# RMSNorm roots with the tokens on partitions, spread by identity matmuls, in a two-layer decoder step on one Trainium2 core

## The chip, the core and the metric

The kernel runs as one launch on one core of one Trainium2 chip. The metric is the device time of the launch in microseconds. Engines: PE is TensorE's matmul (PEld its weight load), DVE is VectorE, ACT is ScalarE, POOL is GpSimd, SP issues the weight transfers.

## The reference, cut to what matters

One step of a two-layer decoder on 320 tokens (256 of a prompt, 64 of eight samples) with D = 2048 features:

```python
def _rmsnorm(x, g):
    y = xf * lax.rsqrt(jnp.mean(xf * xf, axis=-1, keepdims=True) + RMS_EPS)
    return (y * g.astype(jnp.float32)).astype(x.dtype)

def _ffn_sublayer(h, norms_l, w_in, w_out):
    return h + _rmsnorm(_swiglu(_rmsnorm(h, norms_l[2]), w_in, w_out), norms_l[3])

# layer 0
h = h + _rmsnorm(mix, norms_l[1])            # causal pooling mixer
h = _ffn_sublayer(h, norms_l, w_in, w_out)
# shared K/V, then layer 1
kv = _rmsnorm(h, kv_norm) @ w_kv
h = h + _rmsnorm(out, norms_l[1])            # sparse attention, out = o @ w_o
h = _ffn_sublayer(h, norms_l, w_in, w_out)
```

Every sublayer's output is normed before it is added to the residual stream h (a post-norm), and the sum is normed again for the next projection (a pre-norm).

## The kernel before

Features lie on the 128 partitions, in KT = 16 chunks; the NT = 320 tokens lie on the free axis. A projection is made in tiles of 128 output features: for each chunk three fp32r matmuls of 128x320 with the high and low parts of activations and weights (x_hi·w_hi, x_lo·w_hi, x_hi·w_lo; lines 1395 to 1397). SP loads weight panels of 128x2048 into two slots; ACT makes each panel's high part (hi_split, line 492), DVE its low part (lo_split, line 812). The high split of a panel waits until PE has left the panel two before it, which has the same slot. Every engine runs its queue in the order written; semaphores tie them together.

The work around the change is a norm boundary: a post-norm and, behind it, the pre-norm of the next projection. There are three: after the pooling mixer (norms 1 and 2), after the first FFN (3 and 4, ahead of K/V) and after W_O (5 and 6, ahead of the second FFN). Norm 7 ends the kernel. A boundary goes so:

- POOL adds the squares of the 16 output chunks y to acc (line 1282). PE sums them over the partitions with a matrix of ones (acc_sum, lines 1437 to 1442) into PSUM bank STAT, so each of the 128 partitions holds the sums of all 320 tokens. ACT takes the root (rms_root, line 512), DVE the reciprocal (rms_recip, line 820), both of 128x320. In two boundaries PE runs 18 f32 matmuls of 128x128 meanwhile (stay_warm, line 1405).
- For each chunk DVE multiplies y by gain and r (line 850) and adds it to h (line 838). With lag = 1 the add of a chunk stands behind the next chunk's multiplication. ACT then writes x_hi and h times the gain (lines 516 and 598), POOL x_lo (line 1289). All of this is in the unnormed scale: the next projection is multiplied by the pre-norm's r only at its output.
- PE begins at once: four tiles together, chunk by chunk (group, lines 1407 to 1426), 12 matmuls a chunk, one panel for four chunks. I call these panels 1 to 4, and the next two tiles, made in the ordinary way by after_group, the fifth and sixth panel (`tile(c + 4)` and `tile(c + 5)`).
- Meanwhile ACT squares the new h (line 524) and DVE sums the squares (line 864) into acc and r. PE sums these two over the partitions inside the fifth tile, behind its fourth chunk (pre_sum, lines 1444 to 1448), ACT takes the root, DVE the reciprocal. The first readers of r are the FFN's gates (line 1029; ACT's silu, line 536, follows) or the K/V outputs (line 1095). The seventh tile needs the PSUM bank that those reads give back.

The order that matters is written by hand: post_and_pre on ACT (when each panel's high split and each square comes), post_norm on DVE (after which add each low split comes), after_group on PE.

Of the kernel before, what the change touches and what calls it, by code (L numbers as in the profile page):

```python
# [29 lines left out]
P = 128  # L30
# [96 lines left out]
def build(nc, x, st, gains, consts, onehot, rel, w_pool, w_in0, w_in1, w_out0, w_out1, w_kv, w_q, w_o, flips,  # L127
# [86 lines left out]
    pgs = at("pgs", "S", [1, NP_ALL], I32)  # L214
    ident = cst[:, C_ID:C_ID + P]
# [5 lines left out]
    STAT = 7  # L221

    def group_banks(c):

        return 1 - c % 2, 2, 3, 4

    def r_post(c):
# [24 lines left out]
                                                                       "root_made", "r_made"))  # L252
    yn_made, h_made, hacc_made, hg_made = sem("yn_made"), sem("h_made"), sem("hacc_made"), sem("hg_made")
# [228 lines left out]
    def _(act):  # L482
# [108 lines left out]
        def post_and_pre(a, m, k, g, c):  # L591
# [15 lines left out]
            rms_root(m + 1)  # L607

# [188 lines left out]
    def _(dve):  # L797
# [20 lines left out]
        def rms_recip(m, dst=r[:, :]):  # L818
            dve.wait_ge(root_made, m + 1)
            V.reciprocal(dst, root[:, :]).then_inc(r_made, 1)  # L820
            dve.wait_ge(r_made, m + 1)
# [7 lines left out]
        def post_norm(a, m, g, c):  # L829
# [5 lines left out]

            def add(i):
# [9 lines left out]
            rms_recip(m, r_post(c))  # L846
            for i in range(KT):
                if i > lag:
                    dve.wait_ge(h_made, KT * a + i - lag)
                V.scalar_tensor_tensor(out=t_add(i), in0=y[:, i, :], scalar=gn[:, g, i:i + 1],  # L850
                                       in1=r_post(c), op0=ALU.mult, op1=ALU.mult).then_inc(yn_made, 1)
                if i >= lag:
# [3 lines left out]

            for i in range(2, KT):
                if i == 8:
                    lo_split(c + 4, 0)
                dve.wait_ge(sq_made, 16 * m + i + 1)  # L860
                if i >= 4:
                    dve.wait_ge(hacc_made, (KT - 2) * a + i - 3)
# [1003 lines left out]
```

## Time and profile before

| | |
|---|---|
| time, median of 3 runs | 2569.56 us (2568.44 to 2571.85) |
| the profiled execution | 2569.97 us, its span 2568.4 us |
| TensorE busy | 2508.5 us, 98% of the span |
| VectorE busy | 1203.5 us, 47% |
| ScalarE busy | 924.1 us, 36% |
| GpSimd busy | 267.6 us, 10% |
| mean granted TensorE clock | 0.995 |

The share of an engine is its busy time over the span. A wait is shown in the timeline in square brackets behind the instruction it delayed, with the releaser: `[1.88 <-DVE r L864]` is 1.88 us of idling that ended when line 864 on DVE was done. The granted clock is a share of 2.4 GHz; the other level, 1.2 GHz, shows as 0.50.

### The profile page before, as it was taken

The page shows a single profiled execution, that of the slowest core. Times are in us where ns is not written, and L with a number is a line of the kernel's source. Part 1 is how long each engine was busy: PE and PEld are TensorE (multiplying, and loading weights), DVE is VectorE, ACT ScalarE, POOL GpSimd, SP SyncE. Part 2 cuts the span into 40 slices and gives each one's busy share as a digit, 9 for nine tenths or more (in the row PEclk, how much of TensorE's full clock was granted, in tenths as well). Part 3 has the DMA queues.
Part 4 walks back from the last instruction along what each step waited for, and adds up shares of the span by engine and source line. Part 5 has one row for each costly group of instructions (what it writes and reads, how often), then busy time and mean ns, then how long its engine had stood idle before and what let it go on. Part 6 is the DMA issues. An engine that isn't in the chain of part 4 may idle for free.

```text
span 2568.4 us, 43982 instructions
## 1 busy us (share of the span) xinstructions
PE 2508.5 (98%) x17310; PEld 2463.1 (96%) x17310; DVE 1203.5 (47%) x1361; ACT 924.1 (36%) x1154; POOL 267.6 (10%) x316
## 2 busy tenths in 40 slices
PE   6999999999999999999999999999999999999997
PEld 6899999999999999999998799899999999999997
DVE  7564444444444444644534743744444444444444
ACT  4554223323332333532324643633233233323332
POOL 0420000000000001300002311300000000000012
PEclk9999999999999999999999999999999999999998
DMA  6434444344444444456445464344444444444443
GB/s 246 164 131 147 156 162 152 135 162 163 147 155 157 151 153 152 134 159 177 157 165 180 167 185 155 115 147 160 162 147 151 151 159 147 147 162 151 152 149 127
DMA packets 89481, 400.64 MB, mean 156 GB/s; under 512 B 13788, under 2 KB 24428, under 8 KB 59858
## 3 DMA queue, kind: packets, MB, share of 16 engines
q1 hardware_dynamic: 79202, 379.92, 43.9%
q0 software_dynamic: 6160, 12.60, 1.5%
q10 hardware_dynamic: 4064, 7.42, 0.8%
q8 instruction: 31, 0.51, 0.1%
q14 instruction: 24, 0.20, 0.0%
HBM read 392.16 MB, written 19.02 MB: 160 GB/s over the span
## 4 chain that ended last, share of the span: by engine, by line
PE 89%; DVE 5%; ACT 3%; issue 1%; SPq 1%; POOL 1%; DMA 0%; DVEq 0%; ACTq 0%
PE ps L1395 27%; PE ps L1397 27%; PE ps L1396 27%; PE ps L1480 2%; ACT w_hi L492 1%; DVE w_lo L812 1%; PE ps L1649 1%; PE ps L1575 1%; ACT y L598 0%; ACT x_hi L516 0%; PE ps L1646 0%; POOL sc L1360 0%; PE ps L1679 0%; SPq L367 0%; ACT sq L524 0%
## 5 line engine op out<-in xcount | busy, mean ns | idle before, releaser
L1395 PE MATMUL ps<-x_hi,w_hi 128*128 128x320 f32 x3536 | 1095.4, 310 | 5.9 <-DVE sg L1029 2.4
L1396 PE MATMUL ps<-x_lo,w_hi 128*128 128x320 f32 x3536 | 1093.2, 309 | 0.0
L1397 PE MATMUL ps<-x_hi,w_lo 128*128 128x320 f32 x3536 | 1093.1, 309 | 0.0
L812 DVE TENSOR_TENSOR w_lo<-w_raw,w_hi 128x2048 fp32r<-128x2048 f32 (+1 forms) x362 | 744.5, 2057 | 651.3 <-ACT w_hi L492 651.3
L492 ACT CAST w_hi<-w_raw 128x2048 fp32r<-128x2048 f32 (+1 forms) x362 | 618.7, 1709 | 515.4 <-PE ps L1397 479.7
L1395 PEld LDWEIGHTS ps<-x_hi,w_hi 128*128 128x128 f32 x3536 | 664.6, 188 | 8.1 <-issue 3.0
L1396 PEld LDWEIGHTS ps<-x_lo,w_hi 128*128 128x128 f32 x3536 | 664.6, 188 | 0.5 <-issue 0.4
L1397 PEld LDWEIGHTS ps<-x_hi,w_lo 128*128 128x128 f32 x3536 | 664.4, 188 | 0.0
L1397 PE MATMUL ps<-hid_hi,w_lo 128*128 128x320 f32 x1408 | 435.1, 309 | 0.0
L1395 PE MATMUL ps<-hid_hi,w_hi 128*128 128x320 f32 x1408 | 435.1, 309 | 0.0
L1396 PE MATMUL ps<-hid_lo,w_hi 128*128 128x320 f32 x1408 | 435.1, 309 | 0.0
L1395 PEld LDWEIGHTS ps<-hid_hi,w_hi 128*128 128x128 f32 x1408 | 264.4, 188 | 0.0
L1396 PEld LDWEIGHTS ps<-hid_lo,w_hi 128*128 128x128 f32 x1408 | 264.4, 188 | 0.0
L1397 PEld LDWEIGHTS ps<-hid_hi,w_lo 128*128 128x128 f32 x1408 | 264.4, 188 | 0.0
L1301 POOL TENSOR_TENSOR hid_lo<-hb,hid_hi 128x320 f32 x88 | 77.4, 880 | 1586.5 <-ACT hid_hi L540 1586.5
L540 ACT CAST hid_hi<-hb 128x320 f32 (+1 forms) x88 | 40.4, 459 | 408.3 <-DVE hb L1037 408.3
L536 ACT ACTIVATE sg<-sg 128x320 f32<-128x320 f32 x88 | 41.6, 473 | 385.2 <-DVE sg L1029 385.0
L1055 DVE TENSOR_TENSOR y<-y,ps 128x320 f32 (+1 forms) x128 | 62.5, 488 | 201.0 <-PE ps L1397 201.0
L1029 DVE TENSOR_TENSOR sg<-ps,r 128x320 f32<-128x320 f32 x88 | 43.2, 491 | 153.5 <-PE ps L1397 153.4
L1037 DVE TENSOR_TENSOR hb<-sg,ps 128x320 f32<-128x320 f32 x88 | 42.9, 488 | 133.7 <-PE ps L1397 133.0
L503 ACT ACTIVATE sq<-y 128x320 f32<-128x320 f32 x48 | 22.7, 472 | 176.0 <-DVE y L1055 97.3
L1282 POOL TENSOR_TENSOR acc<-acc,sq 128x320 f32<-128x320 f32 x60 | 56.0, 933 | 239.2 <-ACT sq L503 211.6
(253 smaller groups left out, 1471.8 us busy)
## 6 DMA issues: line engine op xcount, KB each, us to landing
w_raw<-w_in_dram SPq DMA_DIRECT2D x176, 1024.0 KB, 4.9
w_raw<-w_out_dram SPq DMA_DIRECT2D x128, 704.0 KB, 4.0
w_raw<-w_kv_dram SPq DMA_DIRECT2D x24, 1024.0 KB, 6.4
w_raw<-w_q_dram SPq DMA_DIRECT2D x17, 1024.0 KB, 4.9
w_raw<-w_o_dram SPq DMA_DIRECT2D x15, 1024.0 KB, 5.5
win_out_dram<-win_kv_dram POOLq DMA_DIRECT2D x8, 992.0 KB, 5.4
rowsK<-cmp_data_dram SPq DMA_DIRECT2D x16, 256.0 KB, 7.1
rowsV<-cmp_data_dram SPq DMA_DIRECT2D x16, 256.0 KB, 4.0
```

The lines of the kernel that those rows point to most:

```text
L492: nc.scalar.copy(w_hi[:, slot, 0:width], src).then_inc(hi_made, 1)
L536: A(sg[:, :], sg[:, :], ACT.Silu).then_inc(silu_made, 1)
L812: V.tensor_tensor(w_lo[:, slot, 0:width], src, w_hi[:, slot, 0:width].bitcast(F32), ALU.subtract).then_inc(lo_made, 1)
L1029: V.tensor_tensor(sg[:, :], ps[:, banks[0], 0:NT], r[:, :], ALU.mult).then_inc(bank_read[c % 2], 1)
L1037: V.tensor_tensor(hb[:, :], sg[:, :], ps[:, banks[1], 0:NT], ALU.mult).then_inc(bank_read[(c + 1) % 2], 1)
L1055: V.tensor_tensor(y[:, n, :], y[:, n, :], ps[:, (o + j) % 2, 0:NT], ALU.add).then_inc(bank_read[(o + j) % 2], 1)
L1282: G.tensor_tensor(acc[:, :], acc[:, :], sq[:, i % 2, :], ALU.add).then_inc(acc_made, 1)
L1301: G.tensor_tensor(hid_lo[:, i, :], hb[:, :], hid_hi[:, i, :].bitcast(F32), ALU.subtract).then_inc(hid_made, 1)
L1395: M(out, wh, xh[:, k, :], start=(k == 0), stop=False)
L1396: M(out, wh, xl[:, k, :], start=False, stop=False)
L1397: last = M(out, wl, xh[:, k, :], start=False, stop=(k == kt - 1))
L1480: return M(ps[:, bank + j // CS, half * w:(half + 1) * w], w1[:, j, :], rows[:, :, j % CS, :], start=(j % CS == 0), stop=(j % CS == CS - 1))
```

## The change

The sums over partitions are turned round: acc (or sq, or r) of 128 tokens becomes the stationary operand and one column of ones the moving one, so that a sum of squares lands with its token on a partition. The 320 tokens need three such thirds (starting at tokens 0, 128 and 192), each one column: root and reciprocal are then of 128x3. To have r on all partitions again, PE multiplies: each of the three columns, broadcast as the stationary operand, with the identity (across_rows, 128 + 128 + 64 columns). For the pre-norms ACT copies the result from PSUM into r (r_kept), which the readers now wait for. Of the 18 matmuls of stay_warm, 4 stand ahead of the spread and 10 behind it, in another bank.

Besides, the first chunk is added before the second is multiplied; ACT's squares and splits and DVE's splits and sums are put in another order; PE sums the squares of the pre-norm behind the eighth chunk of the fifth tile and spreads r behind the twelfth. In the first boundary the spread stands among the matmuls of the block compression.

```diff
+    THIRDS = 0, P, NT - P
+    def third_sum(m):
+        return ps[:, STAT - 2:STAT + 1, 0:1] if m % 2 and m > 1 else ps[:, STAT, NT:NT + 3].unsqueeze(2)
...
         def rms_root(m):
             act.wait_ge(stat_made, m + 1)
-            A(root[:, :], ps[:, STAT, 0:NT], ACT.Sqrt, bias=epsc[:, 0:1], scale=1.0 / D).then_inc(root_made, 1)
+            dst, src = (rootT, third_sum(m)[:, :, 0]) if m else (root[:, :], ps[:, STAT, 0:NT])
+            A(dst, src, ACT.Sqrt, bias=epsc[:, 0:1], scale=1.0 / D).then_inc(root_made, 1)
...
                 A(y[:, i, :], h[:, i, :], ACT.Copy, scale=gn[:, g, i:i + 1]).then_inc(hg_made, 1)
+                if i == 2:
+                    squares_pre(a, 0, 3)
+                if i == 3:
+                    squares_pre(a, 3, 4)
+                if i == 6:
+                    hi_split(c + 2, 0)
                 if i == 9:
-                    hi_split(c + 2, 0)
+                    squares_pre(a, 4, 6)
+                if i == 10:
+                    hi_split(c + 3, 0)
                 if i == 13:
-                    hi_split(c + 3, 0)
-            squares_pre(a, 0, 8)
-            hi_split(c + 4, 0)
-            squares_pre(a, 8, KT)
+                    hi_split(c + 4, 0)
+            squares_pre(a, 6, KT)
             hi_split(c + 5, 0)
             rms_root(m + 1)
+            act.wait_ge(rb_made, m + 1)
+            nc.scalar.copy(r[:, :], ps[:, STAT, 0:NT]).then_inc(r_kept, 1)
...
                 if i == 2:
                     lo_split(c + 1, 0)
-                if i == 11:
+                if i == 8:
                     lo_split(c + 2, 0)
-                if i == 15:
+                    square_sums(2, 4)
+                if i == 12:
                     lo_split(c + 3, 0)
...
+            rms_recip(m)
+            dve.wait_ge(rb_made, m)
+            normed(0)
+            add(0)
+            for i in range(1, KT):
+                normed(i)
                 if i > lag:
                     add(i - lag)
             if lag:
                 add(KT - 1)
...
+            lo_split(c + 4, 0)
+            square_sums(4, KT)
+            rms_recip(m + 1)
             lo_split(c + 5, 0)
-            rms_recip(m + 1)
+            dve.wait_ge(r_kept, a + 1)
...
             def sums(k):
-                if k == 4:
+                if k == 8:
                     pre_sum(m)
+                if k == 12:
+                    across_rows(m, STAT)
...
+        def across_rows(m, bank):
+            pe.wait_ge(r_made, m + 1)
+            done = 0
+            for n, t in enumerate(THIRDS):
+                last = M(ps[:, bank, done:t + P], rT[:, n:n + 1].broadcast_to([P, P]), ident[:, done - t:P],
+                         start=True, stop=True)
+                done = t + P
+            last.then_inc(rb_made, 1)
...
-            M(ps[:, STAT, 0:NT], ones[:, :], acc[:, :], start=True, stop=False)
-            M(ps[:, STAT, 0:NT], ones[:, :], r[:, :], start=False, stop=True).then_inc(stat_made, 1)
+            for n, t in enumerate(THIRDS):
+                M(third_sum(m)[:, n], acc[:, t:t + P], ones[:, 0:1], start=True, stop=False)
+                last = M(third_sum(m)[:, n], r[:, t:t + P], ones[:, 0:1], start=False, stop=True)
+            last.then_inc(stat_made, 1)
...
-        values(0, 20, CB)
+        values(0, 20, 24)
+        pe.wait_ge(b1_made, 2)
+        across_rows(1, P_FFN0 % 2)
+        values(0, 24, CB)
         values(1, 0, CB).then_inc(cmp_sum, 1)
         ffn(P_FFN0, 0, 2, 0)
         acc_sum(3)
-        stay_warm(18)
+        stay_warm(4)
+        across_rows(3, P_KV % 2)
+        stay_warm(10)
         group(P_KV, 1)
...
         ffn(P_FFN1, 3, 6, HT)
         acc_sum(7)
+        across_rows(7, 0)
```

What this moves, at three places. First PE at the second boundary, from the post-norm's sum to the first matmul of the group (cst holds the identity, rt the three columns of root and reciprocal). Before:

```order
L1440 MATMUL ps<-acc,ones 128x320 [waits acc_made]
L1442 MATMUL ps<-sq,ones 128x320 [waits sq_made]
L1405 MATMUL ps<-ones 128x128 x18
L1420 MATMUL ps<-x_hi,w_hi 128x320 [waits xhi_made,lo_made]
L1420 MATMUL ps<-x_hi,w_hi 128x320 x3
```

Now:

```order
L1473 MATMUL ps<-ones,acc 128x1 [waits acc_made]
L1473 MATMUL ps<-ones,acc 128x1 x2
L1478 MATMUL ps<-ones,sq 128x1 [waits sq_made]
L1478 MATMUL ps<-ones,sq 128x1 x2
L1435 MATMUL ps<-ones 128x128 x4
L1486 MATMUL ps<-cst,rt 128x128 [waits r_made]
L1486 MATMUL ps<-cst,rt 128x128
L1486 MATMUL ps<-cst,rt 128x64
L1435 MATMUL ps<-ones 128x128 x10
L1450 MATMUL ps<-x_hi,w_hi 128x320 [waits xhi_made,lo_made]
```

PE now waits for DVE's reciprocal in the middle of its warm-up, and the ten matmuls behind the spread stand ahead of the group.

Then ACT at the end of the same boundary, from the last chunk on. Before:

```order
L516 ACTIVATE x_hi<-h,gn 128x320 [waits h_made]
L598 ACTIVATE y<-h,gn 128x320
L524 ACTIVATE acc<-h 128x320
L524 ACTIVATE r<-h 128x320
L524 ACTIVATE sq<-h 128x320 x2
L524 ACTIVATE sq<-h 128x320 [waits hacc_made] x4
L492 CAST w_hi<-w_raw 128x2048 [waits tile_made,raw_in0]
L524 ACTIVATE sq<-h 128x320 [waits hacc_made] x8
L492 CAST w_hi<-w_raw 128x2048 [waits tile_made,raw_in1]
```

Now:

```order
L525 ACTIVATE x_hi<-h,gn 128x320 [waits h_made]
L607 ACTIVATE y<-h,gn 128x320
L533 ACTIVATE sq<-h 128x320 [waits hacc_made] x10
L500 CAST w_hi<-w_raw 128x2048 [waits tile_made,raw_in1]
L521 ACTIVATE rt<-ps,few 128x3 [waits stat_made]
L624 COPY r<-ps 128x320 [waits rb_made]
```

Ten squares are left behind the last chunk instead of sixteen, and the fifth panel's split, before between them, now stands ahead of the last two chunks; the copy of r stands ahead of whatever ACT does for the next projection.

Last DVE in the same boundary, the middle of the new order (the rows of before have no split between the third chunk and the twelfth):

```order
L872 TENSOR_TENSOR h<-h,ps 128x320 [waits yn_made]
L829 TENSOR_TENSOR w_lo<-w_raw,w_hi 128x2048 [waits hi_made]
L868 TENSOR_TENSOR acc<-acc,sq 128x320 [waits sq_made]
L868 TENSOR_TENSOR r<-r,sq 128x320 [waits sq_made]
L859 SCALAR_TENSOR_TENSOR ps<-y,gn,ps 128x320 [waits h_made]
```

The third panel's low split stands behind the ninth chunk's add, with two sums of squares, and the chunks that follow queue behind them.

## Rows read from the trace of the kernel before

**Rows 1.** The page: busy time of each engine; the chain that ended last.

```profile
PE 2508.5 (98%) x17310; PEld 2463.1 (96%) x17310; DVE 1203.5 (47%) x1361; ACT 924.1 (36%) x1154; POOL 267.6 (10%) x316
...
PE 89%; DVE 5%; ACT 3%; issue 1%; SPq 1%; POOL 1%; DMA 0%; DVEq 0%; ACTq 0%
```

**Rows 2.** Timeline, second boundary: start, duration (us), engine, operation, count [wait <-releaser].

```profile
1054.28 0.81 PE L1442 MATMUL ps<-sq,ones 128*128 128x320 f32 x2 [0.73 <-ACT sq L503]
1054.65 4.26 PEld L1405 LDWEIGHTS ps<-ones 128*128 128x128 f32 x36
1055.12 0.53 ACT L512 ACTIVATE acc<-ps,few 128x320 f32<-128x320 f32 x1 [0.90 <-PE ps L1442]
...
1055.68 2.16 DVE L820 RECIPROCAL ps<-acc 128x320 f32<-128x320 f32 x1 [1.96 <-ACT acc L512]
...
1060.02 0.83 PE L1420 MATMUL ps<-x_hi,w_hi 128*128 128x320 f32 x4 [0.92 <-ACT x_hi L516]
```

**Rows 3.** Single lines over the span: duration ns min/median/max, starts, forms.

```profile
L1214 DVE RECIPROCAL rec<-tot x24: 167/172/193, 1382.9 to 1484.1; 128x6 f32<-128x6 f32 x16, 128x3 f32<-128x3 f32 x8
...
L508 ACT ACT_TABLE_LOAD  x5: 1283/1283/1283, 1.4 to 2475.9; - x5
L508 ACT ACTIVATE few<-few x5: 202/203/203, 2.7 to 2477.2; 128x1 f32<-128x1 f32 x5
...
L1494 PE MATMUL ps<-ones,brow x4: 167/208/250, 53.4 to 97.8; 128*128 128x1 f32 x4
```

**Rows 4.** Timeline: two low parts on POOL, one sum of squares on DVE.

```profile
112.75 0.87 POOL L1289 TENSOR_TENSOR x_lo<-y,x_hi 128x320 fp32r<-128x320 f32 x1 [0.24 <-ACT y L598]
...
1627.26 2.07 POOL L1289 TENSOR_TENSOR x_lo<-y,x_hi 128x320 fp32r<-128x320 f32 x1 [1.83 <-ACT y L598]
...
1083.39 1.17 DVE L864 TENSOR_TENSOR r<-r,sq 128x320 f32<-128x320 f32 x1
```

**Rows 5.** Timeline, PE: the fifth and sixth tile of the second boundary.

```profile
1090.27 0.41 PE L1395 MATMUL ps<-x_hi,w_hi 128*128 128x320 f32 x1 [0.51 <-DVE w_lo L812]
...
1094.17 1.08 PE L1447 MATMUL ps<-acc,ones 128*128 128x320 f32 x2 [1.88 <-DVE r L864]
...
1102.23 0.31 PE L1395 MATMUL ps<-x_hi,w_hi 128*128 128x320 f32 x1
...
1109.12 0.31 PE L1397 MATMUL ps<-x_hi,w_lo 128*128 128x320 f32 x1
```

**Rows 6.** Windows: PE, PEld, DVE, ACT, POOL busy (instructions), clock, DMA share, GB/s.

```profile
1096.00:1097.00 1.00, 1.00 (x5) 0.89 (x4) 1.00 (x1) 0.53 (x1) 0.00 (x0) 0.50 0.00 0
1649.00:1650.00 1.00, 1.00 (x4) 0.71 (x3) 1.00 (x1) 0.13 (x1) 0.00 (x0) 0.50 0.00 0
```

**Rows 7.** Timeline, third boundary: fifth tile, its sums, first read of r, seventh tile.

```profile
1643.52 0.42 PE L1395 MATMUL ps<-x_hi,w_hi 128*128 128x320 f32 x1 [0.52 <-DVE w_lo L812]
...
1647.41 1.36 PE L1447 MATMUL ps<-acc,ones 128*128 128x320 f32 x2 [1.87 <-DVE r L864]
...
1653.04 0.49 DVE L1029 TENSOR_TENSOR sg<-ps,r 128x320 f32<-128x320 f32 x1
...
1663.76 0.42 PE L1395 MATMUL ps<-x_hi,w_hi 128*128 128x320 f32 x1 [1.04 <-DVE sg L1029]
```

**Rows 8.** Timeline, first boundary: third panel's split, fifth tile, r's first reader, later tiles.

```profile
126.15 1.91 ACT L492 CAST w_hi<-w_raw 128x2048 fp32r<-128x2048 f32 x1 [9.03 <-PE ps L1425]
...
147.02 0.31 PE L1395 MATMUL ps<-x_hi,w_hi 128*128 128x320 f32 x1
...
155.08 0.49 DVE L1029 TENSOR_TENSOR sg<-ps,r 128x320 f32<-128x320 f32 x1
...
155.61 0.47 ACT L536 ACTIVATE sg<-sg 128x320 f32<-128x320 f32 x1 [2.94 <-DVE sg L1029]
...
164.47 0.42 PE L1395 MATMUL ps<-x_hi,w_hi 128*128 128x320 f32 x1 [1.36 <-DVE sg L1029]
...
179.78 0.41 PE L1395 MATMUL ps<-x_hi,w_hi 128*128 128x320 f32 x1 [0.95 <-DVE w_lo L812]
```

More of the change, by code:

```diff
@@ L816, in tile_wait, with rms_recip @@
             dve.wait_ge(tile_made, half * 2 + (c + TOFF + 1))
-        def rms_recip(m, dst=r[:, :]):
+        def rms_recip(m):
             dve.wait_ge(root_made, m + 1)
-            V.reciprocal(dst, root[:, :]).then_inc(r_made, 1)
-            dve.wait_ge(r_made, m + 1)
+            if m:
+                V.reciprocal(rT, rootT).then_inc(r_made, 1)
+            else:
+                V.reciprocal(r[:, :], root[:, :]).then_inc(r_made, 1)
+                dve.wait_ge(r_made, m + 1)
         def x_low(k, g, i):
@@ L834, in t_add, with normed, square_sums @@
                 return ps[:, STAT - i % 2 * lag, 0:NT]
+            def normed(i):
+                if i > lag:
+                    dve.wait_ge(h_made, KT * a + i - lag)
+                V.scalar_tensor_tensor(out=t_add(i), in0=y[:, i, :], scalar=gn[:, g, i:i + 1],
+                                       in1=r_post(c), op0=ALU.mult, op1=ALU.mult).then_inc(yn_made, 1)
+            def square_sums(lo, hi):
+                for i in range(lo, hi):
+                    dve.wait_ge(sq_made, 16 * m + i + 1)
+                    if i >= 4:
+                        dve.wait_ge(hacc_made, (KT - 2) * a + i - 3)
+                    total = (acc, r)[i % 2][:, :]
+                    V.tensor_tensor(total, total, sq[:, i % 2, :], ALU.add).then_inc(hacc_made, 1)
             def add(i):
@@ L855, in post_norm @@
                 add(KT - 1)
[L857 to L862, printed above, removed]
-                total = (acc, r)[i % 2][:, :]
-                V.tensor_tensor(total, total, sq[:, i % 2, :], ALU.add).then_inc(hacc_made, 1)
+            lo_split(c + 4, 0)
+            square_sums(4, KT)
+            rms_recip(m + 1)
             lo_split(c + 5, 0)
-            rms_recip(m + 1)
+            dve.wait_ge(r_kept, a + 1)
         def last_norm(a, m, g):
-            rms_recip(m, r_post(0))
+            rms_recip(m)
+            dve.wait_ge(rb_made, m)
             t_add = ps[:, STAT, 0:NT], ps[:, STAT - 1, 0:NT]
@@ L1404, in stay_warm @@
             for _ in range(n):
-                M(ps[:, 5, 0:P], ones[:, :], ones[:, :], start=True, stop=True)
+                M(ps[:, 4, 0:P], ones[:, :], ones[:, :], start=True, stop=True)
         def group(c, k):
@@ L1439, in acc_sum @@
             pe.wait_ge(acc_made, KT * (m // 2 + 1))
-            M(ps[:, STAT, 0:NT], ones[:, :], acc[:, :], start=True, stop=False)
+            for n, t in enumerate(THIRDS if m > 1 else ()):
+                M(third_sum(m)[:, n], acc[:, t:t + P], ones[:, 0:1], start=True, stop=False)
             pe.wait_ge(sq_made, KT * m)
-            M(ps[:, STAT, 0:NT], ones[:, :], sq[:, (KT - 1) % 2, :], start=False, stop=True).then_inc(stat_made, 1)
+            for n, t in enumerate(THIRDS):
+                if m == 1:
+                    M(third_sum(m)[:, n], acc[:, t:t + P], ones[:, 0:1], start=True, stop=False)
+                last = M(third_sum(m)[:, n], sq[:, (KT - 1) % 2, t:t + P], ones[:, 0:1], start=False, stop=True)
+            last.then_inc(stat_made, 1)
[7 more added lines that the diff above has]
+            last.then_inc(rb_made, 1)
         def pre_sum(m):
             pe.wait_ge(hacc_made, (KT - 2) * (m // 2))
-            M(ps[:, STAT, 0:NT], ones[:, :], acc[:, :], start=True, stop=False)
-            M(ps[:, STAT, 0:NT], ones[:, :], r[:, :], start=False, stop=True).then_inc(stat_made, 1)
+            for n, t in enumerate(THIRDS):
+                M(third_sum(m)[:, n], acc[:, t:t + P], ones[:, 0:1], start=True, stop=False)
+                last = M(third_sum(m)[:, n], r[:, t:t + P], ones[:, 0:1], start=False, stop=True)
+            last.then_inc(stat_made, 1)
         def x_ready(k):
@@ L1752, in _ @@
         acc_sum(5)
-        stay_warm(18)
+        stay_warm(4)
+        across_rows(5, P_FFN1 % 2)
+        stay_warm(10)
         ffn(P_FFN1, 3, 6, HT)
         acc_sum(7)
+        across_rows(7, 0)
     block_ctx.close()
```

9 lines of the change are left out of this document (3 added, 6 removed).

## The prediction

> **What bounds the kernel now.** Read first the busy times and the chain that ended last [rows 1]: TensorE works for 98% of the span and makes 89% of the chain, so the other engines cost time only where TensorE waits for them. The windows and the timeline show where: in four norms. Of a post-norm and the pre-norm behind it (I call the pair a boundary) there are three, and one post-norm ends the kernel. So the sum has four terms, each read from its own stage. A change of 0.2% is 5.1 us, and a measurement of this kernel tells no less from no change.
>
> **Prices.** The reciprocal of 128x320 takes 2.16 us [rows 2]; of 128x3 it takes 0.17 [rows 3]. The square root of 128x320 takes 0.53 [rows 2], ScalarE's smallest operation 0.20 [rows 3]; I take 0.24 for 128x3. An f32 matmul loads its weights twice: 36 loads of warm-up last 4.26 us [rows 2], 0.118 each with the tail of the last; I take 0.116. The f32 matmuls of one column last 0.17 to 0.25 each by their rows [rows 3], so 0.08 to 0.125 a load: the bounds. Three matmuls are 0.70 us (0.5 to 0.75), six 1.39 (1.0 to 1.5). Copying the spread root, 128x320, costs as the 0.53 root.
>
> **Second boundary (after the first FFN, ahead of K/V).** Before, the root's sum is there at 1055.09, the root ends at 1055.65, the reciprocal at 1057.84, and the first matmul of the group starts at 1060.02 [rows 2]. Now: sum (0.70 + 0.15 tail) at 1055.1 again, root and reciprocal done at 1055.6, four warm-up matmuls until 1055.9, the spread 0.70 + 0.15, so r at 1056.7: 1.15 earlier. Adding the first chunk at once, not behind the second's 0.46, makes it 1.6; less 0.15 for one hand-over more, 1.45. But the ten other warm-up matmuls hold TensorE for 20 x 0.116 = 2.3 us, to 1058.9. The group starts 1.1 earlier. Its next stop is chunk 1's low part, which GpSimd makes behind VectorE's split of the second panel; that split begins 1.0 earlier, so 1.0 is kept.
>
> Inside the group the splits of panels 3, 4 and 5 move ahead among the chunks. A low part alone takes 0.87; one that begins during a split took 2.07 [rows 4], 1.2 more, and ends 0.74 behind the split. I followed the new order through the group with these durations and TensorE's 1.76 a chunk (12 matmuls at 0.1466). ScalarE reaches the fourth panel behind chunk 10, VectorE's half ends at 1080.35, so low part 11 is ready at 1081.09; TensorE wants it at 1080.7, 0.4 late. The fifth panel's split ends at 1086.39 and holds low part 14 to 1087.13, wanted at 1086.4: 0.8 late. Before, both panels were split behind those chunks and neither low part was late. The moved sums of squares 2 and 3 meet GpSimd too: one such sum took 1.17 [rows 4], and of that I count 0.3 inside the 0.4. The Trainium skill, in "SBUF — State Buffer", section "🔬 SBUF: two separate sides", says that a VectorE instruction with two SBUF inputs and a GpSimd one lock each other out whole. By it both sums could be held a full low part, an estimate of 2 x 0.87 = 1.7 us with the row's duration, and this term would be 1.4 worse.
>
> In return the fifth panel's split is due long before its tile: the wait of 0.51 and 0.2 of stalls at 1090.27 go [rows 5]. The tile starts at -1.0 + 1.2 - 0.7 = 0.5 earlier. Of its two tiles' 96 matmuls the last starts 1109.12 - 1090.27 = 18.85 behind the first; at the pitch of the undisturbed sixth tile, (1109.12 - 1102.23)/47 = 0.1466 [rows 5], that would be 13.93. The 4.9 between are the wait of 1.88, the sums and what follows them. The windows show that [rows 6]: the granted clock is 0.50, 1.2 GHz, behind the wait. Less 1.88 and about 1.3 for the sums at full clock, 1.7 are the fall's. Now the squares are made among the chunks, their sums stand at about 1092.5, and TensorE asks for them after eight chunks (1089.8 + 3.5 = 1093.3): no wait, no fall. Sums of 1.39 and a spread of 0.70 stand in place of the 4.9, so 2.8 less. **Term: -3.3.**
>
> **Third boundary (after W_O, ahead of the second FFN).** The tile again starts 0.5 earlier. Before, the FFN's first read of r came 1653.04 - 1643.52 = 9.52 behind it [rows 7], with the wait of 1.87 and a fall like the other's. Now it comes after eight chunks 3.52 + sums 1.39 + four chunks 1.76 + spread 0.70 + tail 0.15 + copy 0.53 = 8.05: 1.5 earlier. The work from that read to the seventh tile (1663.76 - 1653.04 = 10.72, all on VectorE and ScalarE) stays, so the tile resumes 2.0 earlier. But TensorE reaches it 14.08 (96 matmuls) + 1.39 + 0.70 = 16.17 after the fifth's start and waits until 8.05 + 10.72 = 18.77: the wait grows from 1.04 to 2.6. Waits of 1.88 and 1.87 were followed by the half clock, one of 1.36 was not [rows 5, 7, 8]; so I expect a new fall, +1.7. **Term: -0.3**; -2.0 if the clock holds.
>
> **First boundary (pooling layer, ahead of the first FFN).** VectorE's saving is hidden: TensorE is busy with compression matmuls until the group starts. It gets 0.70 of spread, and 0.2 for the sum, whose 1.39 stand against two matmuls of 320 columns (one lasts 0.81 [rows 2], and they overlap): +0.9. ScalarE stands for 9.03 us at the third panel's split, at 126.15 [rows 8], until TensorE has left the first panel. It stood there after ten chunks, now after seven, with all that is behind it in its queue. That makes the same two low parts late, by 0.5 and 0.9: +1.4. The tile of 147.02 starts 2.3 later. r follows 8.05 behind it, as before (155.08 - 147.02 = 8.06). But the gate's table load of 1.28 [rows 3] and its activation, before at 155.61, 0.53 behind the first read [rows 8], now stand behind the copy of r: 1.28 between copy and activation, +0.75. The seventh tile resumes +3.0 after 164.47, with its wait up from 1.36 to 2.1. If the clock falls there, 1.7 more is mostly taken up by the wait of 0.95 at 179.78. **Term: +3.0** (2.0 to 4.0).
>
> **End.** The last normalisation stands behind root 0.53 and reciprocal 2.16, as in rows 2. Now 0.24 + 0.17 + 0.85 for the spread and two hand-overs of 0.1 stand there: **-1.2**. The square-root table doesn't move; the weight transfers keep their order on SP's queue and can only start earlier, with the splits that free their slots.
>
> **Sum.** -3.3 - 0.3 + 3.0 - 1.2 = -1.8 against the profiled execution's 2569.97, which gives 2568.2; the median of the runs, 2569.56, is 0.4 lower, which would give 2567.8. The forecast between them is **2568.0 us**: no change that can be measured.
>
> **Rivals.** *Low parts in time* (faster). If GpSimd and VectorE miss each other, the three lots of 1.2 to 1.4 in the groups go (3.9), and the third boundary's clock holds (1.7): 2568.0 - 5.6 = 2562.4. For it: in the trace only some low parts are held. Against: the splits are closer together now. Chance 0.25.
>
> *One-column matmuls don't hold the clock* (slower). They keep TensorE loading weights while few columns pass. If such stretches are as idle to the clock as a wait, it falls behind the sums of both later post-norms and of three pre-norms: 5 x 1.7 = 8.5, 2576.5. [...] Against: by themselves they are no longer than the 1.36 after which the clock stayed [rows 8]. The Trainium skill ("TensorE: Matmul & The Clock Gate", section "🔬 Part 1: The HAM clock gate") says that recent activity of the array sets the clock; no row here shows what a one-column matmul counts for. Chance 0.08.
>
> *It doesn't do what it says*: the squares still end late, because ScalarE stands at the third panel's split, and TensorE waits at the sums for a microsecond with the clock's fall kept. Then the wait of about 1 and the fall's 1.7 are back in the second boundary, 2.7 (the third has its new fall in the sum already): 2570.7. My margin there is only 0.7 us. Chance 0.17.
>
> **How the numbers follow.** Forecast 0.5, rivals 0.25, 0.08 and 0.17. The range takes in the first and third rival and the bounds of the loads (+-0.4 in each of four terms) and of the first boundary: 2562.0 to 2573.0. Faster by over 0.2% (below 2564.4) is the first rival, 0.25; slower (above 2574.7) the second, 0.08; the rest 0.67.
>
> **What would show it.** Right: no wait for sums of squares in the second and third boundary and a granted clock of 1.00 behind them; waits on GpSimd's low parts near chunks 11 and 14 of each group; a wait of 2.6 and then 0.50 at the seventh tile of the third; the last norm starting 1.2 nearer to its sum. Wrong: a fall of the clock behind one-column sums, a wait at them, a spread that takes over 0.9, or groups without late low parts.

## The result: 0.14% slower, and the profile after

The changed kernel takes 2574.16 us (median of 18 runs, 2571.81 to 2577.51) against 2570.35 for the kernel before in the same runs: a ratio of 1.0014, 95% interval 1.0008 to 1.0021, so 2 to 5 us more. It is slower, by less than the 0.2% that the prediction took as its bound, and 1.2 us above the range's end of 2573.0. The execution that was profiled is the slowest of the 18, 2577.51 us: its stages below add up to 5.9 us more than those of before, while the medians differ by 3.8.

To compare executions I cut each profile at four places: the *first* boundary runs from the post-norm's first sum to the seventh tile, the *second* from the last chunk's sum to the first matmul behind the sixth tile, the *third* from the last chunk's sum to the seventh tile, the *end* from the last chunk's sum to the end of the span. What lies between is the same in both kernels (first FFN 889.8, K/V to W_O 498.15, second FFN 888.4 us), and what lies ahead of the first sum, where all kernels here are the same, differs by up to 5 us between executions (95.7 to 100.9), so profiled spans alone mislead.

| us | first | second | third | end |
|---|---|---|---|---|
| before | 66.56 | 55.08 | 56.25 | 16.26 |
| after | 71.51 | 56.55 | 57.05 | 14.98 |
| difference | +4.95 | +1.47 | +0.80 | -1.28 |
| predicted | +3.0 | -3.3 | -2.0 | -1.2 |

The prediction's -0.3 for the third boundary is -2.0 up to the seventh tile and a fall of the clock, +1.7, behind it. Only the end went as forecast. The first boundary of the kernel after, in its timeline (start, duration, engine, operation, count, and in brackets the wait and what ended it; rows of several engines together):

```profile
131.60 3.15 POOL L1319 TENSOR_TENSOR x_lo<-y,x_hi 128x320 fp32r<-128x320 f32 x2 [15.49 <-ACT y L607]
...
132.85 1.17 DVE L868 TENSOR_TENSOR acc<-acc,sq 128x320 f32<-128x320 f32 x1
133.94 1.16 DVE L868 TENSOR_TENSOR r<-r,sq 128x320 f32<-128x320 f32 x1
...
137.04 0.82 ACT L533 ACTIVATE sq<-h 128x320 f32<-128x320 f32 x2
...
138.67 1.90 ACT L500 CAST w_hi<-w_raw 128x2048 fp32r<-128x2048 f32 x1
...
140.47 0.56 ACT L525 ACTIVATE x_hi<-h,gn 128x320 fp32r<-128x320 f32 x1
140.60 2.29 DVE L829 TENSOR_TENSOR w_lo<-w_raw,w_hi 128x2048 fp32r<-128x2048 f32 x1 [1.18 <-ACT w_hi L500]
...
141.08 0.85 PE L1450 MATMUL ps<-x_hi,w_hi 128*128 128x320 f32 x4
...
141.56 2.88 POOL L1319 TENSOR_TENSOR x_lo<-y,x_hi 128x320 fp32r<-128x320 f32 x2 [1.83 <-ACT y L607]
...
143.66 0.85 PE L1455 MATMUL ps<-x_lo,w_hi 128*128 128x320 f32 x4 [1.15 <-POOL x_lo L1319]
...
148.97 1.15 DVE L868 TENSOR_TENSOR acc<-acc,sq 128x320 f32<-128x320 f32 x1
...
149.83 0.85 PE L1455 MATMUL ps<-x_lo,w_hi 128*128 128x320 f32 x4 [0.63 <-POOL x_lo L1319]
150.05 1.17 DVE L868 TENSOR_TENSOR r<-r,sq 128x320 f32<-128x320 f32 x1
...
152.28 0.31 PE L1425 MATMUL ps<-x_hi,w_hi 128*128 128x320 f32 x1
...
156.41 0.38 PE L1495 MATMUL ps<-ones,acc 128*128 128x1 f32 x2 [0.45 <-DVE r L868]
...
160.43 0.43 ACT L624 COPY r<-ps 128x320 f32<-128x320 f32 x1 [2.22 <-PE ps L1486]
160.87 1.28 ACT L545 ACT_TABLE_LOAD   x1
...
171.03 0.41 PE L1425 MATMUL ps<-x_hi,w_hi 128*128 128x320 f32 x1 [1.78 <-DVE sg L1059]
```

Behind the third panel's split VectorE makes the moved sums of squares 2 and 3. Both run beside two of GpSimd's low parts and take 1.17 and 1.16; beside no low part such a sum takes 0.49 (sum 6 of the kernel before, at 140.79). VectorE's next multiplication starts at 135.02. Then ScalarE makes two squares and the fourth panel's high split before chunk 11's high part, which ends at 141.03: TensorE starts that chunk at 141.08. Its low part is held by VectorE's split until 143.5, and chunk 14's again at 149.8. The fifth tile starts at 152.28, 31.05 behind the group's start at 121.22; before it was 147.02 - 118.68 = 28.34. Then sums 4 and 5 take 1.15 and 1.17 beside GpSimd's last low parts, and TensorE waits 0.45 for the last sum at 156.41. Before, it waited 0.51 behind the fifth tile's fourth chunk:

```profile
149.45 0.81 PE L1447 MATMUL ps<-acc,ones 128*128 128x320 f32 x2 [0.51 <-DVE r L864]
```

The copy of r is ahead of the gate's table load, as forecast, and the seventh tile waits 1.78 (before 1.36, [rows 8]).

TensorE in the second boundary, which answers to [rows 2] and [rows 5]:

```profile
1060.82 0.83 PE L1478 MATMUL ps<-ones,sq 128*128 128x1 f32 x6 [0.70 <-ACT sq L511]
1061.51 2.06 PE L1435 MATMUL ps<-ones 128*128 128x128 f32 x8
1063.36 1.38 PE L1486 MATMUL ps<-cst,rt 128*128 128x128 f32 x6
...
1066.93 0.83 PE L1450 MATMUL ps<-x_hi,w_hi 128*128 128x320 f32 x4
...
1071.12 0.87 PE L1455 MATMUL ps<-x_lo,w_hi 128*128 128x320 f32 x4 [1.01 <-POOL x_lo L1319]
...
1090.42 0.85 PE L1455 MATMUL ps<-x_lo,w_hi 128*128 128x320 f32 x4 [1.15 <-POOL x_lo L1319]
...
1096.46 0.85 PE L1455 MATMUL ps<-x_lo,w_hi 128*128 128x320 f32 x4 [0.49 <-POOL x_lo L1319]
...
1103.04 0.38 PE L1495 MATMUL ps<-ones,acc 128*128 128x1 f32 x2 [0.45 <-DVE r L868]
```

and in the third, which answers to [rows 7]:

```profile
1616.22 1.14 PE L1435 MATMUL ps<-ones 128*128 128x128 f32 x8
1617.19 0.78 PE L1486 MATMUL ps<-cst,rt 128*128 128x128 f32 x6
...
1643.65 0.87 PE L1455 MATMUL ps<-x_lo,w_hi 128*128 128x320 f32 x4 [1.15 <-POOL x_lo L1319]
...
1656.28 0.38 PE L1495 MATMUL ps<-ones,acc 128*128 128x1 f32 x2 [0.47 <-DVE r L868]
...
1672.58 0.41 PE L1425 MATMUL ps<-x_hi,w_hi 128*128 128x320 f32 x1 [1.90 <-DVE sg L1059]
```

The same eight loads of warm-up take 2.06 in the second and 1.14 in the third, the same spread 1.38 and 0.78. The windows show why (TensorE's granted clock is the third value from the end):

```profile
1062.40:1063.40 1.00, 1.00 (x7) 1.00 (x7) 0.00 (x0) 1.00 (x1) 0.00 (x0) 0.50 1.07 416
...
1106.00:1107.00 1.00, 1.00 (x6) 1.00 (x6) 1.00 (x1) 0.00 (x0) 0.00 (x0) 0.50 0.00 0
...
1617.00:1618.00 1.00, 1.00 (x12) 1.00 (x11) 0.00 (x0) 1.00 (x1) 0.00 (x0) 1.00 0.14 41
...
1660.00:1661.00 1.00, 1.00 (x7) 1.00 (x6) 0.46 (x1) 0.00 (x0) 0.00 (x0) 0.50 0.00 0
```

The clock falls to 0.50 behind the post-norm's sums in the second boundary but not in the third, and behind the pre-norm's sums in both. Each fall takes 1.71 us of clock (the sum of one minus the clock over its windows of 1 us, 1061 to 1065, 1105 to 1110, 1658 to 1663). Before there were two, at [rows 6]. At the end the last normalisation starts 2.31 behind the last sum (2563.27 - 2560.96), before 3.6.

### The profile page after: what moved, and what is told of

The parts are those of the page before. It is cut to its first block, busy times and chain, and to the rows that moved or that the text cites. A ratio compares the mean times of both kernels' runs of the same rounds, so it can differ in the third digit from the quotient of the medians.

```text
span 2575.9 us, 44151 instructions
## 1 busy us (share of the span) xinstructions
PE 2515.7 (98%) x17392; PEld 2473.2 (96%) x17392; DVE 1194.8 (46%) x1361; ACT 922.9 (36%) x1157; POOL 271.8 (11%) x316
## 4 chain that ended last, share of the span: by engine, by line
PE 90%; DVE 5%; ACT 3%; issue 1%; POOL 1%; SPq 1%; DMA 0%; DVEq 0%; ACTq 0%
PE ps L1425 27%; PE ps L1426 27%; PE ps L1427 27%; PE ps L1529 2%; DVE w_lo L829 1%; ACT w_hi L500 1%; PE ps L1703 1%; DVE r L868 1%; PE ps L1629 1%; ACT sq L533 0%; PE ps L1700 0%; POOL sc L1390 0%; PE ps L1733 0%; SPq L375 0%; PE ps L1774 0%
```

## The experiments

Two theories for what the forecast lacked. *Order*: the new places of the splits and squares make high and low parts late. *Clock*: one-column sums let the clock fall. All ratios are to the kernel before, run beside each on the same chip (its medians there 2569.2 to 2569.8). "Falls" are those of the clock inside the boundaries and just behind them, in the one profiled execution; the mean clock is that of all timed executions, where one fall takes off 1.71/2570 = 0.0007, and is known to some 0.0002. It counts falls elsewhere too: ahead of the first sum TensorE waits for a tile gathered by DMA, and behind that wait the 14 profiles have no fall, one or two, in kernels that are the same up to there.

| kernel | us | ratio, 95% | first | second | third | falls | mean clock |
|---|---|---|---|---|---|---|---|
| before | 2570.35 | | 66.56 | 55.08 | 56.25 | 2 | 0.9960 |
| after | 2574.16 | 1.0014, 1.0008 to 1.0021 | 71.51 | 56.55 | 57.05 | 3 | 0.9959 |
| after again | 2574.61 | 1.0016, 1.0006 to 1.0025 | 73.06 | 53.50 | 57.51 | 2 | 0.9956 |
| roots, old order | 2567.59 | 0.9987, 0.9978 to 0.9996 | 68.07 | 53.03 | 53.98 | 2 | 0.9954 |
| order alone | 2582.39 | 1.0041, 1.0027 to 1.0055 | | 57.50 | | 2 | 0.9960 |
| sums of 64 columns | 2572.92 | 1.0012, 1.0003 to 1.0021 | 71.51 | 53.51 | 55.95 | 1 | 0.9962 |
| splits alone moved | 2575.34 | 1.0016, 1.0007 to 1.0025 | 71.50 | 54.78 | 56.10 | 4 | 0.9946 |
| squares alone moved | 2571.80 | 1.0006, 0.9997 to 1.0015 | 68.07 | 53.27 | 55.16 | 3 | 0.9946 |
| old order, 64 columns, silu | 2561.54 | 0.9968, 0.9956 to 0.9980 | 67.32 | 51.53 | 52.68 | 0 | 0.9975 |
| second split later | 2561.18 | 0.9966, 0.9954 to 0.9978 | 67.33 | 51.53 | 52.71 | 0 | 0.9977 |
| third split earlier | 2564.04 | 0.9977, 0.9968 to 0.9986 | 68.59 | 51.54 | 52.71 | 0 | 0.9970 |
| first norm wide | 2562.25 | 0.9971, 0.9959 to 0.9982 | 67.66 | 51.56 | 52.73 | 0 | 0.9973 |
| old order, silu | 2563.64 | 0.9974, 0.9965 to 0.9984 | 67.32 | 51.54 | 52.71 | 0 | 0.9967 |
| all that helped | 2561.93 | 0.9968, 0.9956 to 0.9981 | 66.40 | 51.53 | 52.70 | 0 | 0.9973 |

In "order alone" the sixth tile waits too, so that two stages don't compare and are left out.

**The changed kernel again.** No edit.

> The changed kernel once more. Two theories. Order: the new places of the splits make low parts late (about 2.2 us in each of three groups) and the sums of squares late (0.45 each), whatever the clock does. Clock: one-column sums let the granted clock fall, 1.6 us each time. Both expect 2572 to 2577 us. Order expects the same waits at the same chunks (about 1.15 and 0.6 at chunks 11 and 14). Clock expects that the places of the falls change from execution to execution (three in the profile: behind the post-norm sum of the second boundary, behind the pre-norm sums of the second and third), and the time with them.

The low parts are late at the same chunks by the same amounts (1.14 and 0.62, 1.14 and 0.49, 1.15 and 0.49), the sums by 0.45 three times. The falls moved: behind the pre-norm's sums of the first boundary (not there in the other execution) and of the third, none in the second, which is 3.05 shorter for two falls fewer. So the lateness is fixed by the program, the falls are not.

**The roots by tokens with the old order.**

```diff
-                if i == 2:
-                    squares_pre(a, 0, 3)
...
-                if i == 6:
-                    hi_split(c + 2, 0)
                 if i == 9:
-                    squares_pre(a, 4, 6)
+                    hi_split(c + 2, 0)
...
+            squares_pre(a, 0, 8)
+            hi_split(c + 4, 0)
+            squares_pre(a, 8, KT)
```

and on VectorE the low splits and sums in their old places; the sums stay behind the eighth chunk.

> The roots by tokens, the spread and the early first add stay; ScalarE's splits and squares and VectorE's splits and sums stand where they stood before. Order expects no low part late at chunks 11 and 14, the fifth panel's wait of 0.5 back, and -2.2 - 0.45 + 0.7 = about -2 in each boundary: 2574.2 - 6 = 2568. Clock expects the falls behind the one-column sums to stay and no more than 1 us from the order: 2573.

2567.59, 7.0 less than the change run beside it (2574.61) and faster than before. TensorE's waits in its timeline:

```profile
1092.86 0.42 PE L1419 MATMUL ps<-x_hi,w_hi 128*128 128x320 f32 x1 [0.51 <-DVE w_lo L823]
...
1096.75 0.38 PE L1489 MATMUL ps<-ones,acc 128*128 128x1 f32 x2
...
1616.51 0.85 PE L1449 MATMUL ps<-x_lo,w_hi 128*128 128x320 f32 x4 [1.16 <-POOL x_lo L1313]
...
1661.66 0.64 PE L1419 MATMUL ps<-x_hi,w_hi 128*128 128x320 f32 x1 [2.35 <-DVE sg L1053]
```

No low part is late but chunk 1's, which was late before too; the fifth panel's 0.5 is back; the sums are in time, with waits of 0.12 or less. The groups are 28.34, 30.25 and 30.40 long (change: 31.05, 31.97, 32.11). The seventh tile of the third boundary waits 2.35, and behind that the clock falls, as the prediction had it for the change. This run decides for the order as the greater cause.

**The new order alone**, put into the kernel before: the same splits, squares and sums, 320 wide, at the eighth chunk, and the wide reciprocal ahead of the sixth panel's split.

> The kernel before with the new order alone: splits, squares and sums at the new places, the wide sums of squares behind the eighth chunk, the wide reciprocal ahead of the sixth panel's split; no roots by tokens, no spread. Order expects low parts late at chunks 11 and 14 and about 2 us lost in the first boundary, 1.8 gained in the second (the wait of 1.88 and the fall gone against the late parts), -0.1 to +1.6 in the third: 2570 to 2572. Clock, if the late low parts were only a small part, expects no fall at the wide sums and a gain: 2565.

2582.39, 10 above the expectation. The groups are those of the change, 31.08, 31.97 and 31.97, without any root by tokens. But the run is no clean test, since I had made a new wait:

```profile
1087.77 0.85 PE L1434 MATMUL ps<-x_lo,w_hi 128*128 128x320 f32 x4 [1.15 <-POOL x_lo L1298]
...
1102.34 2.15 DVE L826 RECIPROCAL r<-acc 128x320 f32<-128x320 f32 x1 [2.00 <-ACT acc L512]
...
1107.27 0.41 PE L1404 MATMUL ps<-x_hi,w_hi 128*128 128x320 f32 x1 [2.02 <-DVE kvT L1104]
```

The reciprocal of 2.15 stands ahead of the sixth panel's split, so the sixth tile is late by 2.02 in all three boundaries, with a fall behind two. Ahead of that split a reciprocal must be as small as the change's 0.17.

**Sums of 64 columns.**

```diff
+    SUM_W = 64
...
-        return ps[:, STAT - 2:STAT + 1, 0:1] if m % 2 and m > 1 else ps[:, STAT, NT:NT + 3].unsqueeze(2)
+        return ps[:, STAT - 2:STAT + 1, 0:SUM_W] if m % 2 and m > 1 else ps[:, STAT, NT:NT + 3 * SUM_W].rearrange(
+            "p (n w) -> p n w", w=SUM_W)
...
-                M(third_sum(m)[:, n], acc[:, t:t + P], ones[:, 0:1], start=True, stop=False)
+                M(third_sum(m)[:, n], acc[:, t:t + P], ones[:, 0:SUM_W], start=True, stop=False)
```

> The changed kernel, but each sum over partitions multiplies 64 columns of ones instead of one; root and reciprocal read one column of the 64. The loads bound these matmuls, so their pitch should stay near 0.11 us a load. Clock expects no fall behind the sums: 2574.2 less 1.6 for one to three falls, 2571 (2569.5 to 2572.5). Order expects no change, 2574, with the same late low parts.

TensorE at the second boundary's post-norm sum:

```profile
1060.04 0.88 PE L1480 MATMUL ps<-ones,sq 128*128 128x64 f32 x6 [0.64 <-ACT sq L513]
1060.76 1.11 PE L1437 MATMUL ps<-ones 128*128 128x128 f32 x8
```

Sixty-four columns cost about what one does (0.88 against 0.83), and no fall follows any sum, though the pre-norm sums wait 0.45 as in the change; the one fall is behind the third seventh tile's wait of 2.37. The time is 1.7 below that of the change run beside it, one fall; the intervals overlap, so timing alone doesn't show it. The mean clock went up by 0.0005 before rounding, which is less than a fall and within twice its uncertainty.

**Splits alone, squares alone.** Two halves of the new order.

```diff
                 if i == 13:
                     hi_split(c + 4, 0)
-            squares_pre(a, 6, KT)
+            squares_pre(a, 0, KT)
```

with no squares among the chunks; and

```diff
+                    squares_pre(a, 4, 6)
                     hi_split(c + 2, 0)
                 if i == 13:
                     hi_split(c + 3, 0)
+            squares_pre(a, 6, 8)
+            hi_split(c + 4, 0)
+            squares_pre(a, 8, KT)
```

with the first four squares behind chunks 2 and 3.

> The changed kernel with only the splits of the panels at the new places; all sixteen squares stand behind the chunks again on ScalarE, their sums behind the fifth panel's split on VectorE. If the splits make the low parts late: waits of about 1.15 and 0.6 at chunks 11 and 14 of each group as in the changed kernel, the groups 31.1 to 32.1 us long. The squares then end later than in the changed kernel, TensorE waits some 2 to 3 us for their sums and the clock falls: about 2580. If the squares were what made them late: groups of 28.4 and 30.3, 2570.

> The changed kernel with only the squares and their sums at the new places; the splits of panels 3, 4 and 5 stand where they stood before. If the splits make the low parts late: groups of 28.4 and 30.3 us as with the whole old order (2567.6), sums ready ahead of time, 2566 to 2568. If the squares and sums among the chunks make them late: waits at chunks 11 and 14 as in the changed kernel, 2573.

Both expectations were wrong. With the splits alone only one low part behind chunk 1 is late, chunk 14's, by 0.41 (groups 29.02, 29.15 and 30.34); the fourth panel's low half starts 16.69 behind the first group's start, against 19.37 in the change; the squares then end so late that the sums wait 1.51. With the squares alone no low part behind chunk 1 is late, but in the second and third boundary the third panel's split is, behind two sums on VectorE (0.63 and 1.16) and two squares on ScalarE (0.82). The rows of both, the splits' first:

```profile
135.16 2.29 DVE L823 TENSOR_TENSOR w_lo<-w_raw,w_hi 128x2048 fp32r<-128x2048 f32 x1 [0.65 <-ACT w_hi L500]
...
145.05 0.85 PE L1448 MATMUL ps<-x_lo,w_hi 128*128 128x320 f32 x4 [0.41 <-POOL x_lo L1312]
...
152.69 0.38 PE L1488 MATMUL ps<-ones,acc 128*128 128x1 f32 x2 [1.51 <-DVE r L862]
```

```profile
1074.29 2.29 DVE L828 TENSOR_TENSOR w_lo<-w_raw,w_hi 128x2048 fp32r<-128x2048 f32 x1 [1.64 <-ACT w_hi L500]
...
1076.63 0.85 PE L1451 MATMUL ps<-x_hi,w_hi 128*128 128x320 f32 x4 [1.99 <-DVE w_lo L828]
```

So the loss at chunk 11 comes from what both together put ahead of it in two queues. Of the 2.7 in the first boundary's group, the splits alone make 0.7 (29.02 - 28.34); the squares alone make nothing there, the two together the rest. In the third boundary the squares alone lose 1.55 (31.95 against 30.40), at the third panel, and the splits alone nothing.

**Old order, 64 columns, silu's table ahead.** To the second experiment's kernel the sums of 64 columns are added, and

```diff
             rms_root(m + 1)
+            if c != P_KV:
+                A(epsr[:, :], epsc[:, :], ACT.Silu)
             act.wait_ge(rb_made, m + 1)
```

> The run with the roots by tokens and the old order (2567.6), with sums of 64 columns and with silu's table loaded (a small activation) ahead of the wait for the spread r. Clock theory: no fall behind the sums; and with the table load of 1.28 out of the way the seventh tile of the third boundary waits 1.1 instead of 2.35, so no fall there either: 0.8 to 1.3 in the first boundary, 1.3 + 1.7 in the third, 0 to 1.7 in the second: 2567.6 - 4.5 = 2563 (2562 to 2564.5). If the table load were hidden: 2567.

2561.54, 8 us faster than before, and 0.5 below the range expected. ScalarE and then TensorE in the third boundary:

```profile
1643.38 1.28 ACT L620 ACT_TABLE_LOAD   x1
1644.67 0.20 ACT L620 ACTIVATE few<-few 128x1 f32<-128x1 f32 x1
1645.52 0.42 ACT L622 COPY r<-ps 128x320 f32<-128x320 f32 x1 [0.64 <-PE ps L1484]
...
1655.42 0.42 PE L1423 MATMUL ps<-x_hi,w_hi 128*128 128x320 f32 x1 [1.09 <-DVE sg L1057]
```

The table is loaded while ScalarE waits; the seventh tile's wait is 1.09 instead of 2.35, and no fall follows. The third boundary is 52.68 (53.98 with the fall of 1.7 just behind it), the first 0.75 shorter.

**Old order with silu's table alone**, sums of one column.

> The run with the roots by tokens and the old order (2567.6) with silu's table loaded ahead of the wait, and sums of one column again. Table load on the path: from r's sums to the seventh tile 13.8 instead of 14.5 in the first boundary, 13.9 instead of 15.2 in the third, and no fall of the clock behind the third's wait: 2567.6 - 0.75 - 1.3 - 1.7 = 2564. The rest to 2561.5 (sums of 64 columns too) is then the falls behind one-column sums: 1.7 us in some executions and not in others.

2563.64, with a mean clock of 0.9967 against the 0.9954 of the same kernel without the early table load: two falls' worth. The stages of the profiled execution, which happened to have no fall in a boundary, are those of the run before to 0.03 us. What is left between the two, 2.1 us, is not in the program's waits. The mean clocks, 0.9967 and 0.9975, differ by about one fall per execution (0.0008 x 2565 = 2.1 us). Where these falls lie is not shown: the two profiled executions differ by 3.9 us, all of it ahead of the first sum, where the kernels are the same. There TensorE waited for the gathered tile as long in the one as in the other, and this run had two falls behind the wait, the run before none:

```profile
87.97 11.91 PE L1525 MATMUL ps<-rowsV,w1V 128*128 128x256 f32 x40 [2.81 <-DMA rowsV<-cmp_data_dram]
```

```profile
87.06 8.90 PE L1527 MATMUL ps<-rowsV,w1V 128*128 128x256 f32 x40 [2.78 <-DMA rowsV<-cmp_data_dram]
```

So this pair says nothing sure of one-column sums; the falls counted at the sums themselves say more, and stand below.

**The second panel's split later**, behind chunk 4's add instead of chunk 2's, and then **the third's earlier**:

```diff
-                if i == 2:
+                if i == 4:
                     lo_split(c + 1, 0)
-                if i == 11:
+                if i == 9:
                     lo_split(c + 2, 0)
```

the first of the two edits in the first run, both in the second, with the high split behind chunk 7 for 9.

> The run before this one with VectorE's split of the second panel behind the add of chunk 4 instead of chunk 2. Order theory: a low part is late only where it starts beside a split; chunk 1's (waits of 1.03 and 1.16, about 1.9 us longer groups in the second and third boundary) then starts ahead of it, so these groups shorten from 30.3 to 28.4: 3.8 less than the run before, 2559. If chunk 1 waits for something else, no change.

> The run with the second panel's split behind chunk 4, and the third panel's splits two or three places earlier (high behind chunk 7, low behind the add of chunk 9, ahead of its old place behind 9 and 11). Queue theory (what a group loses is set by how much stands ahead of the next panel's split in VectorE's and ScalarE's queues): the wait of 1.22 at the third panel goes and no low part is late, groups of 28.4 to 28.9 instead of 30.4 in the second and third boundary, 2561.2 - 3.5 = 2557.7. If the loss only moves on again, to the fourth panel or to a low part: 2561, with a wait there.

Two misses. Chunk 1 is no longer late, but a panel is, the third in the one run and the fourth in the other, and the second and third boundary's groups stay at 30.4; in the second run the first boundary's group also grows, from 28.34 to 29.12, as its fifth panel is late by 0.55:

```profile
1626.18 0.85 PE L1448 MATMUL ps<-x_hi,w_hi 128*128 128x320 f32 x4 [1.21 <-DVE w_lo L827]
```

```profile
1634.80 0.85 PE L1448 MATMUL ps<-x_hi,w_hi 128*128 128x320 f32 x4 [1.21 <-DVE w_lo L827]
```

The wait of 1.2 goes to whichever part stands behind the moved one. In the second and third boundary VectorE starts only with the group, so it has 16 chunks and four splits to do in the group's time; moving them shifts the loss and doesn't remove it.

**The first post-norm wide again**, on top of that and on top of the fastest run.

```diff
-            dst, src = (rootT, third_sum(m)[:, :, 0]) if m else (root[:, :], ps[:, STAT, 0:NT])
+            dst, src = (rootT, third_sum(m)[:, :, 0]) if m > 1 else (root[:, :], ps[:, STAT, 0:NT])
...
-        across_rows(1, P_FFN0 % 2)
```

> The run before this one with the post-norm of the first boundary alone made as in the kernel before: sum, root and reciprocal 320 wide, no spread among the compression's matmuls. TensorE's 1.3 us there go, and VectorE's longer reciprocal stays hidden behind the compression: 1.0 to 1.3 less than the run before, groups as there. If the spread had been hidden: no change.

> The fastest run so far (old order, sums of 64 columns, silu's table ahead of the wait, 2561.5) with the first boundary's post-norm as in the kernel before. From the earlier run of that edit: 0.9 less in the first boundary (66.4 us from its first sum to the seventh tile instead of 67.3), all else the same: 2560.6. If that gain is lost in the first boundary's group, as VectorE starts it later: 2561.5.

The first boundary is 0.93 shorter in both (67.66 for 68.59, 66.40 for 67.32), as expected; in the time of the second, 2561.93 against 2561.54 measured apart from it, that is below what can be told. The fastest form is one of these, some 8 us below the kernel before.

## Why the prediction was wrong

The sum was -1.8 and the measured difference is +3.8. **The step that failed first** is the price of the two moved sums of squares: "one such sum took 1.17 [rows 4], and of that I count 0.3 inside the 0.4". In the trace both take 1.17 and 1.16, in all three boundaries and in both executions of the change; VectorE goes on 2.17 behind the first one's start (135.02 - 132.85), where two of 0.49 make 0.98. That is 1.2 more, and 0.3 was counted. The fourth panel's split starts later by it, and chunk 11 lost 1.7 us in each group (in the first 0.4 at its high part, 1.4 at its low part: 143.66 less 141.08 and eight matmuls' 1.17) for the "0.4" or 0.5 of the prediction. Chunk 14 lost 0.9, 0.8 and 0.8, as forecast. The groups grew by 2.71, 1.71 and 1.85, where the terms had +1.4, +0.6 and +0.6: 3.7 us, all of it chunk 11's. The stretched sums are 0.9 of the 1.3 in each group; the rest is not taken apart (ScalarE's two squares, 0.82 at 137.04, stand ahead of the same split). The old order gives the loss back, as the runs showed.

The Trainium skill ("SBUF — State Buffer", section "🔬 SBUF: two separate sides") lets an instruction of VectorE with two SBUF inputs and one of GpSimd lock each other out whole. The trace agrees: the second sum ends 0.35 behind GpSimd's two low parts (135.10 and 134.75), and where the prediction worked out 1.4 more by that rule, chunk 11 came out 1.3 worse.

**The margin of 0.7 at the sums** went the same way: sums 4 and 5, behind the fifth panel's split, took 1.15 and 1.17, 1.3 more than two of 0.49. The wait of 0.45 in three boundaries, 1.35, was not in the sum. This is the third rival's step, at half its wait.

**The falls.** The prediction let two falls go and put one new one at the third seventh tile: one fewer, -1.7. The profile has three, and the mean clock of all runs is that of before (0.9959 and 0.9960): none fewer. That the clock falls behind one-column sums was the second rival, given 0.08. Its mechanism came true in part, at two or three places in an execution and not at five, and the profiles show a wait with each. Behind pre-norm sums of one column that waited 0.12 or less no fall came (nine sums, of the old order with and without silu and of the squares alone); behind those that waited 0.45 four came in six (the change, twice); behind those that waited 1.51 three in three (the splits alone). So "no wait, no fall" held, and "no wait" was the error.

The width of the sums shows too: after the same 0.45, 64 columns had no fall in three and 320 (the order alone) none in three; behind the second boundary's post-norm sum, with waits of 0.64 to 0.70, one column had a fall in four executions of six and 64 columns in none of six. These are counts of few executions, and chance has a part in them: behind the waits of 2.8 for the gathered tile one execution had two falls and another none. The Trainium skill ("TensorE: Matmul & The Clock Gate", section "🔬 Part 1: The HAM clock gate") says that recent activity of the array sets the clock; the runs agree, in that 64 columns in the same time had no fall behind them. What a one-column matmul counts for is not shown; only the falls are counted. The pre-norm's sums last 1.50 (156.41 to 157.91; forecast 1.39), longer than the 1.36 that the prediction set against them.

Right were: the pitch of the loads and the chain of root, reciprocal and spread (the third boundary's group starts 4.49 behind the sum instead of 5.74, -1.25 for the -1.1 forecast); the end (-1.28 for -1.2); the copy ahead of the table load (+0.75 in the first boundary, which the silu run took back exactly); and the seventh tile's wait in the third boundary (1.90, and 2.35 without the order, for 2.6), with a fall behind it in the three executions that waited 2.35 to 2.37 there and had none 10 us ahead. In the first boundary the spread and sums cost TensorE 0.9 from the first sum on; forecast 0.9. A fall behind the first seventh tile, "mostly taken up" in the prediction, came in the run of the squares alone, and its first FFN was only 0.3 longer (890.10).

In figures: without their falls the boundaries of the change stand at +4.95, +0.13 (the second: 53.50 in the execution without a fall, against 55.08 less 1.71), +0.80 (one fall in both) and -1.28, together +4.6; the forecast without its falls was -0.1. Of the 4.7 between, the groups are 3.7 and the waits for sums, 1.35, more than the rest. The one fall that was to go and did not is another 1.7; the two together, 6.4, are a little more than the 5.6 between -1.8 and +3.8, whose own interval is 2 to 5.

## What to carry to other kernels

When a move puts an instruction beside one that it is known to meet, count the whole stretch that a row shows, here 1.17 for 0.49, for every such instruction. Where several engines feed one another in order, a move is priced by what stands behind it in every queue it passes, taken together and not queue by queue; if a group already waits for one part, as chunk 1 here, there is no slack, and an earlier place for one thing is a later place for another. Make a matmul that only sums as wide as its weight load hides: here 64 columns cost about what one does, and no fall of the clock followed them in the executions profiled. And load an activation table while its engine waits anyway: an edit of two lines took the roots in the old order from 2567.59 to 2563.64.

## What the runs showed of the hardware

- A fall of the granted clock to 0.50 (1.2 GHz) takes the same each time, 1.71 us of clock in the 19 falls in and behind the boundaries of these profiles, though part of it can hide behind a later wait. Its place differs between executions of one program: behind the post-norm's sums of the second boundary in one execution of the change, behind the pre-norm's sums of the first in the other.
- The same wait need not bring a fall. Ahead of the first sum TensorE waits 2.0 to 3.4 us for a gathered tile in every execution; the 40 matmuls behind it then take 8.90 us in five executions (no fall of the clock) and up to 11.91 in the others (one fall or two).
- An f32 matmul with 128 stationary columns costs about the same for 1, 64 and 128 moving columns: three in 0.83, 0.88 and 0.78 us (the spread, its last with 64 columns).
- A sum of squares on VectorE (128x320, both inputs in SBUF) that takes 0.49 beside none of GpSimd's low parts took 1.15 to 1.17 beside one.
- The stages between the boundaries repeat closely (first FFN 889.79 to 889.82 us, second 888.38 to 888.67, where no fall lies behind the boundary), while the stretch ahead of the first sum differs by 5 us: 95.7 to 97.1 with no fall in it, 97.9 to 99.5 with one, 99.9 to 100.9 with two. Single profiled spans of these kernels can't be compared to better than that, their stages can.
